# Two of eleven blocks of a down projection by seven products of squares

## What is computed

```python
def hybrid_layer(x, ...):
    h = rms_norm(x, g_attn_pre)
    proj = jnp.einsum('bsd,de->bse', h, w_in) + b_in
    # ... two groups of heads, each with its own mask and norm ...
    x = x + rms_norm(jnp.einsum('bse,ed->bsd', mix, w_out), g_attn_post)
    h = rms_norm(x, g_ffn_pre)
    f = jax.nn.silu(jnp.einsum('bsd,df->bsf', h, w_gate)) * jnp.einsum('bsd,df->bsf', h, w_up)
    x = x + rms_norm(jnp.einsum('bsf,fd->bsd', f, w_down), g_ffn_post)
    return x
```

## Time and profile before

| | |
|---|---|
| median of 3 runs | 571.66 us (571.55 to 571.73) |
| span of the profiled execution | 569.7 us |
| PE, weight loads, DVE, ACT, POOL busy | 99%, 81%, 66%, 52%, 40% |
| granted TensorE clock | 0.999 of full speed |
| loaded | 105.7 MB |

### The profile page before, as it was taken

How to read it: one execution, slowest core, us unless ns; L and a number is a source line. 1 busy time by engine, 2 the same in 40 slices (tenths; PEclk the granted TensorE clock), 3 DMA queues, 4 the chain that set the end, 5 groups by cost and what they waited for, 6 DMA issues and landing times.

```text
span 569.7 us, 8885 instructions
## 1 busy us (share of the span) xinstructions
PE 562.0 (99%) x3395; PEld 462.1 (81%) x3395; DVE 375.1 (66%) x487; ACT 294.0 (52%) x420; POOL 229.1 (40%) x451
## 2 busy tenths in 40 slices
PE   8999999999999999999999999999999999999996
PEld 5878878888888888888888878888888888888884
DVE  5799895946755746365597987775855746734622
ACT  6576684664445353263546748574645354425420
POOL 1101001507797797860120000033296797785000
PEclk9999999999999999999999999999999999999999
DMA  8954624538556461478266443525575455352701
GB/s 299 370 210 156 237 89 173 223 133 315 184 217 202 167 221 33 189 294 298 89 239 208 158 167 124 211 76 221 222 258 201 173 217 183 113 221 88 282 1 74
DMA packets 18730, 107.34 MB, mean 188 GB/s; under 512 B 2816, under 2 KB 3072, under 8 KB 7168
## 3 DMA queue, kind: packets, MB, share of 16 engines
q1 hardware_dynamic: 18688, 106.78, 50.8%
HBM read 105.72 MB, written 1.05 MB: 187 GB/s over the span
## 4 chain that ended last, share of the span: by engine, by line
PE 93%; DVE 3%; DMA 1%; ACT 1%; issue 1%; POOL 0%; SPq 0%; DVEq 0%; POOLq 0%
PE bank L1209 84%; PE bank L1249 4%; PE bank L1234 2%; PE bank L1275 2%; PE bank L1302 2%; DVE w_l L812 1%; DMA raw<-in_w_blocks 1%; ACT work L631 0%; DVE work L896 0%; DVE work L874 0%; DVE work L897 0%; DVE work L952 0%; DVE work L902 0%; DVE x L986 0%; ACT work L608 0%
## 5 line engine op out<-in xcount | busy, mean ns | idle before, releaser
L812 DVE TENSOR_TENSOR w_l<-raw,w_h 128x2048 fp32r<-128x2048 f32 x90 | 206.6, 2301 | 112.6 <-ACT w_h L559 112.4
L559 ACT ACTIVATE w_h<-raw 128x2048 fp32r<-128x2048 f32 x90 | 171.7, 1915 | 108.5 <-PE bank L1209 91.5
L1209 PE MATMUL bank<-w_h,actT_h 128*128 128x512 f32 (+1 forms) x568 | 223.9, 394 | 0.1
L517 POOL COPY work<-work 32x128 f32<-32x128 f32 (+1 forms) x384 | 191.3, 498 | 75.6 <-DVE work L1013 59.8
L1209 PE MATMUL bank<-w_h,actT_l 128*128 128x512 f32 (+1 forms) x568 | 219.9, 387 | 0.0
L1209 PE MATMUL bank<-w_l,actT_h 128*128 128x512 f32 (+1 forms) x568 | 219.4, 386 | 0.0
L1209 PEld LDWEIGHTS bank<-w_h,actT_h 128*128 128x128 f32 x568 | 106.8, 188 | 23.1 <-issue 2.5
L1209 PEld LDWEIGHTS bank<-w_h,actT_l 128*128 128x128 f32 x568 | 106.7, 188 | 22.1
L1209 PEld LDWEIGHTS bank<-w_l,actT_h 128*128 128x128 f32 x568 | 106.9, 188 | 20.1
L504 POOL TENSOR_TENSOR norms<-norms,constants 128x1 f32<-128x1 f32 x8 | 2.7, 342 | 131.7 <-ACT bank L658 131.7
L1209 PE MATMUL bank<-w_h,fT_h 128*128 128x512 f32 x160 | 49.4, 390 | 0.0
(11 more groups left out here) (78 smaller groups left out, 396.1 us busy)
## 6 DMA issues: line engine op xcount, KB each, us to landing
raw<-in_w_blocks SPq DMA_DIRECT2D x90, 1024.0 KB, 4.8
bias<-in_b_in SPq DMA_DIRECT2D x8, 256.0 KB, 6.1
raw<-in_w_blocks SPq DMA_DIRECT2D x4, 256.0 KB, 5.9
raw<-in_w_blocks SPq DMA_DIRECT2D x2, 512.0 KB, 8.6
x<-in_x SPq DMA_DIRECT2D x2, 512.0 KB, 10.7
gain_b<-in_g_attn_post SPq DMA_DIRECT2D x2, 512.0 KB, 7.3
bias<-in_g_ffn_pre SPq DMA_DIRECT2D x2, 512.0 KB, 7.4
gain_b<-in_g_ffn_post SPq DMA_DIRECT2D x2, 512.0 KB, 6.5
```

The costliest lines, as they stand in the source:

```text
L517: ins = nc.gpsimd.tensor_copy(crossed[t][32 * j:32 * j + 32, i * n:(i + 1) * n], squares[t][32 * i:32 * i + 32, j * n:(j + 1) * n])
L559: nc.scalar.activation(w["h"][:, slot(b), :], raw[:, r, :], ACT.Copy).then_inc(hi_ready, 1)
L812: nc.vector.tensor_tensor(w["l"][:, slot(b), :], raw[:, slot(b, RAW), :], w["h"][:, slot(b), :].bitcast(F32), ALU.subtract).then_inc(lo_re ...
L1209: ins = nc.tensor.matmul(bank[BANK_OF[name]][:, 0:n], left[s][:, at + k, tokens(t)], right[r][:, k, c * BANK:c * BANK + n], start=first an ...
```

## The change

A block of the down projection is X = A B with A of 2 x 2 tiles (tokens by k, 128 x 128) and B of 2 x 2 tiles (k by columns, 128 x 512). Strassen's scheme in Winograd's form makes X with seven products instead of eight, out of sums of tiles of A and of B. It is applied to the k-tiles 0 to 3 (chunk 0 of f), in two of the eleven blocks.

- The down blocks come in another order: k-tiles 4 to 9 (35 to 37), then the first fast block as two entries, `raw` (38: three tiles of B, high and low part of 1536 columns) and `sum` (39: four sums of tiles, 2048 columns), then k-tiles 10 to 13 (40, 41), the second fast block (42, 43), and 14 to 21 (44 to 47). There are 48 entries, 46 of them loaded; slots and raw buffers go round without leaving any out.
- DVE makes the sums of weights (`add_squares`) and of f (`add_s`, in chunk 1 of gate and up, with `hi_s` and `lo_s`). POOL's exchange of chunk 1 waits for `add_s`.
- PE accumulates four of the seven products straight in banks of the result or of their own, and three into banks 4 to 7 over both fast blocks. After the second, ACT copies one of them (`keep_m1`), and DVE joins them to the four banks of the result (`join_first`, `join_second`, eight operations in PSUM).
- PE's order at the end: half of block 44 for tile 1; tile 0 of 44, each bank once its join is made; 45 to 47 for tile 0; the rest for tile 1, with the next layer's transposes in the middle of 46.
- Some buffers move (silu and squares change places, the sums lie over the gains or the work buffer), and the next layer's `gain_a` is loaded later.

```diff
-BLOCKS += [("down", k, 2, 0, D) for k in range(0, KF, 2)]
+FAST = 2
+FAST_CHUNKS = FAST // 2
+BLOCKS += [("down", k, 2, 0, D) for k in (4, 6, 8)]
+RAW_AT = []
+for n in range(FAST):
+    RAW_AT += [len(BLOCKS)]
+    BLOCKS += [("raw", 2 * n, 2, 0, D), ("sum", 2 * n, 2, 0, D)]
+    if n == 0:
+        BLOCKS += [("down", k, 2, 0, D) for k in (10, 12)]
+FIRST_LATE = len(BLOCKS)
+BLOCKS += [("down", k, 2, 0, D) for k in (14, 16, 18, 20)]
...
@@ scalar
                 hi_f(L, FFN_CHUNKS - 2, 0)
+                after(L, FIRST_DOWN)
                 hi_f(L, FFN_CHUNKS - 2, 1)
-                for b in range(FIRST_DOWN, NB - 4):
+                for b in range(FIRST_DOWN + 1, NB - 4):
+                    if b == RAW_AT[FAST - 1]:
+                        keep_m1(L)
                     after(L, b)
-                    if b == FIRST_DOWN + 4:
+                    if b == RAW_AT[0] + 1:
                         hi_f(L, FFN_CHUNKS - 1, 0)
                         hi_f(L, FFN_CHUNKS - 1, 1)
...
@@ vector
+            def add_s(L, c):
...
+                nc.vector.tensor_tensor(s3, a11, a21, ALU.subtract)
+                link(L, nc.vector.tensor_tensor(s1, a21, a22, ALU.add))
+                link(L, nc.vector.tensor_tensor(s2, s1, a11, ALU.subtract))
+                nc.vector.tensor_tensor(s4, a12, s2, ALU.subtract).then_inc(s_added, 1)
...
+            def add_squares(L, n):
...
+                link(L, nc.vector.tensor_tensor(dst[:, 0, :].rearrange("p (a n) -> p a n", a=2),
+                                                raw[:, r, BANK:3 * BANK].rearrange("p (a n) -> p a n", a=2),
+                                                b12.unsqueeze(1).broadcast_to([P, 2, BANK]), ALU.subtract))
+                link(L, nc.vector.tensor_tensor(dst[:, 1, 0:BANK], dst[:, 0, BANK:2 * BANK], b11, ALU.add))
+                nc.vector.tensor_tensor(dst[:, 1, BANK:2 * BANK], b21, dst[:, 1, 0:BANK], ALU.subtract
+                                        ).then_inc(sums_ready, 1)
...
+                first, second = RAW_AT
+                lo_f(L, FFN_CHUNKS - 2, 0)
+                squares_f(L, FFN_CHUNKS - 1, 0)
+                add_squares(L, 0)
+                after(L, FIRST_DOWN)
+                lo_f(L, FFN_CHUNKS - 2, 1)
+                squares_f(L, FFN_CHUNKS - 1, 1)
+                after(L, FIRST_DOWN + 1)
+                after(L, FIRST_DOWN + 2)
+                after(L, first)
+                add_squares(L, 1)
+                after(L, first + 1)
+                lo_f(L, FFN_CHUNKS - 1, 0)
+                lo_f(L, FFN_CHUNKS - 1, 1)
+                after(L, first + 2)
+                after(L, first + 3)
+                join_first(L)
+                after(L, second)
+                after(L, second + 1)
+                join_second(L)
...
@@ tensor
+                product(m1, a11, b11, first, last)
+                product(x12, s4, b22, False, last)
+                product(x11, a12, b21, False, last).then_inc(block_used, 1)
+                pe.wait_ge(lo_ready, L * NB + b + 2)
+                ends = [product(m6, s2, t2, first, last), product(m5, s1, t1, first, last),
+                        product(m7, s3, t3, first, last)]
+                product(x21, a22, t4, False, last).then_inc(block_used, 1)
...
+                multiply(L, 1, FIRST_LATE, (0,), asks=True).then_inc(second_begun, 1)
+                multiply(L, 0, FIRST_LATE, asks=False, apart=True)
+                f_landed(L, FFN_CHUNKS - 2, 0)
+                multiply(L, 0, FIRST_LATE + 1)
+                multiply(L, 0, FIRST_LATE + 2)
+                f_landed(L, FFN_CHUNKS - 1, 0)
+                multiply(L, 0, FIRST_LATE + 3)
+                pe.wait_ge(joined, 4 * L + 4)
+                multiply(L, 1, FIRST_LATE, (1,))
+                multiply(L, 1, FIRST_LATE + 1)
+                multiply(L, 1, FIRST_LATE + 2, (0,))
+                if L < depth - 1:
+                    rows(L + 1, 0, 0)
+                multiply(L, 1, FIRST_LATE + 2, (1,))
+                f_landed(L, FFN_CHUNKS - 1, 1)
+                multiply(L, 1, FIRST_LATE + 3)
```

More of the change, by code:

```diff
@@ L70, with slot, before, load_count @@
 SLOTS = 4
[L71 to L83, removed]
+SUMS = 2
+def slot(L, b):
+    return (L * NB + b) % SLOTS
+def before(b):
+    return b - SLOTS
+def load_count(L, b):
+    return L * NL + LOADED.index(b)
+def raw_slot(L, b):
+    return load_count(L, b) % RAW
+def raw_done(L, b):
+    return (load_count(L, b) // RAW + 1) * 16
 def freed_by(b):
@@ L95, in completes @@
     m, k0, nk, col, n = BLOCKS[b]
-    if m == "down":
+    if m in ("down", "raw", "sum"):
         return [("down", t, c) for c in range(2)] if k0 + nk == KF else []
@@ L222, in trunk @@
         minus_half, eps = constants[:, 0:1], constants[:, 1:2]
-        junk = [[silu[t].bitcast(BF16) for t in range(T)], [rope_tmp.bitcast(BF16)] * T]
+        junk = [[squares[t].bitcast(BF16) for t in range(T)], [rope_tmp.bitcast(BF16)] * T]
         bank = [ctx.enter_context(nc.psum_tensor(f"bank{b}", [P, BANK], F32)) for b in range(8)]
+        products = [bank[b] for b in (4, 5, 6, 7)]
         x_in_done = [sem(f"x_in_done{t}") for t in range(T)]
@@ L394, in _ @@
             for L in range(depth):
-                for b in range(RAW + 1, NB):
+                for b in LOADED[RAW + 1:]:
                     load_block(L, b)
@@ L547, in hi @@
             def hi(L, b, wait=True):
[L549 to L550 removed]
+                m, k0 = BLOCKS[b][0:2]
+                if m == "sum":
+                    act.wait_ge(sums_ready, sums_done(L, k0 // 2))
+                else:
+                    r = raw_slot(L, b)
+                    act.wait_ge(raw_in[r], raw_done(L, b))
                 last = before(b)
@@ new lines, in join, with join_first @@
+            def join(L, t, c, what):
+                x = bank[BANK_OF["down", t, c]]
+                nc.vector.tensor_tensor(x[:], x[:], what, ALU.add).then_inc(joined, 1)
+            def join_first(L):
+                _, m6, m5, _ = products
+                dve.wait_ge(m1_kept, L + 1)
+                join(L, 0, 0, m1_sum)
+                dve.wait_ge(products_full, 3 * L + 1)
+                link(L, nc.vector.tensor_tensor(u2, m1_sum, m6[:], ALU.add))
+                dve.wait_ge(products_full, 3 * L + 2)
+                link(L, nc.vector.tensor_tensor(u4, u2, m5[:], ALU.subtract))
+                join(L, 0, 1, u4)
```

235 lines of the change are left out of this document (168 added, 67 removed).

## The result

| | before | after |
|---|---|---|
| median of the runs | 571.68 us | 580.70 us (580.26 to 580.92) |
| ratio | | 1.0158 (95% interval 1.0144 to 1.0173) |
| span of the profiled execution | 569.7 us | 578.5 us |
| PE, DVE, ACT, POOL busy | 99%, 66%, 52%, 40% | 97%, 70%, 52%, 44% |

The account below looks back on a forecast made before the run. PE's number of products was taken to bound the kernel. Waits of 2.3 + 2.2 us in layer 0 and 1.6 + 2.2 - 1.36 in layer 1 gave +6.9, taken as +6.8: 571.66 -> 578.5 us, range 570.2 to 581.5.

Parts of the forecast that it names:

- The products: PE, both layers: each fast block takes 21 products for 24, twelve fewer at 0.2267 us, 2.72 us in all.
- Layer 0's saving is worth nothing: Start of layer 1: PE reaches block 3 earlier by 1.36 us but waits for DVE's chain until the same 296.04.
- Rival 2: Exchange in time and layer 0's saving kept too, because DVE's chain moves: 568.9 us; chance 0.04.
- Rivals 3: Rival 3: PE alone counts, sums and joins cost two short waits of 0.5 us a layer: 571 to 575; chance 0.07.
- 4: Rival 4: block 40 and the exchange both late, over 581.5 us; chance 0.04.
- The hold-up of POOL by the new sums: Last exchange, down projection: 17 locked DVE instructions (24.1 us) hold up POOL's copies, adding 19.0 us to its 19.0.
- The short form of the sum: Last exchange's length from whole terms, less 0.3 for each passing copy: 38.0 us, ending at 259.5 and 536.6.
- Rival 1: Down projection: exchange in time as the new sums don't hold POOL up or run faster, 570.3 us; chance 0.15.
- The start of that group: Chunk 4's exchange starts about 1.7 us later in layer 0 and 2.6 in layer 1, from chunk 1's added work.
- The waits at 44: Down projection: block 44 ready at 264.8 and 542.3, wanted at 262.5 and 540.7; PE waits 2.3 and 1.6 us.
- The joins: Down projection, behind block 44: PE waits 1.5 us at the first join and 0.7 after, 2.2 in each layer.
- the likeliest case: Whole kernel: late exchange makes PE wait at block 44 and the joins, 578.5 us, bounds 575.5 to 580.5; chance 0.70.

Follow-up runs that it names:

- The transposes: Changed kernel with DVE's three sums of weights of each fast block made stream transposes of 1024, 512 and 512 columns: 574.25 us, ratio 1.0059.
- the edit that shortens the chain: Layer 1: block 3's low half before the rotation, its first products before projection 0's transposes; on changed kernel with f-late and drains-first edits 569.13 us, on kernel before 571.27.

## Why the prediction was right, and where not

- **The products** come at 0.2267 us, twelve less: right, and the run of six left out in layer 1 shows 1.15 of the 1.36.
- **Layer 0's saving is worth nothing**, since DVE's chain gates block 3 of layer 1: right, forecast as a gap of 1.3, measured 1.29, and shown by leaving six products out there (1.0001) and by the edit that shortens the chain only where the saving exists (0.9959 with it, 0.9998 without). Rival 2 is out. Rivals 3 (571 to 575) and 4 (over 581.5) are out by the time, 580.70.
- **The hold-up of POOL by the new sums**: right in kind and size. From the last group's start to the last copy I had 38.7 and 39.1 us, it takes 38.96 and 38.97. The transposes settle it: with them, the last group is 3.4 us shorter. The short form of the sum took 0.3 us off for each copy that passes where its test on layer 1 had taken 0.2; by the measured 38.96 it is (24.1 + 19.0 - 38.96) / 17 = 0.24. Of DVE's added work the prediction had some 18 us a layer; it is (405.7 - 375.1) / 2 = 15.3. Rival 1 is out; its price, about 571 for sums that don't hold POOL up, is not what that run shows (574.25), because the late start and the gap at the start stay with it.
- **The start of that group** is the term that was mis-sized: 1.7 and 2.6 us later by the forecast, 2.7 and 4.3 measured. I had priced what chunk 1's extra work costs there and taken it that the ring then goes on at its old pace. It doesn't: exchange, ACT's and DVE's halves of f, the product with silu and the transpose follow one another in a ring (18.4 to 19.0 us of copies and 3.39 to the next start) that is as long as PE's chunk of 21.8 us. In the kernel before, layer 1, it ran with it, 18.37 + 3.39. In the changed kernel each further chunk takes 22.4 us, so that lateness grows by 0.6 a chunk instead of going away. In layer 1 that makes 1.4 and 1.7 us from chunk 0 to 1 and from 1 to 2, where I had 1.3 and 1.2, and then 0.6 twice. The slower rhythm isn't the change's own, since the kernel before falls into it in some layers too; of the profiled kernels, each with the sums of f goes in it behind chunk 1 in both layers. Against a ring that keeps PE's pace (87.06 us) the changed kernel's last group is 4.7 us late in layer 0 as well; the 2.7 counts from a layer 0 that was itself 2.0 late. A low half of f of 0.77 us lies beside the second exchange there (at 213.46, in layer 0) and behind it in the kernel before (at 492.36, when the copies of the group of 474.22 were all but through). In layer 0 of the kernel before, which goes in the slower rhythm, it lies beside it too (at 214.11). That this is where the 0.6 comes from was not tried.
- **The gap at the start of the down projection** (2.11 and 1.75 us) is the step that is missing. I followed the late exchange forward to block 44 and not through DVE's queue in chunk 5, where the drains that PE needs stand behind two low halves that it doesn't need yet. The kernel before had 0.25 us from the drain's end to PE's load there, so a look at who ends last ahead of 225.79 would have shown that nothing covers it.
- **The waits at 44**: 2.3 and 1.6 forecast, 1.29 and 1.31 measured. The exchange ended later than I had it, at 260.72 for 260.2 in layer 0, but PE came later too, by what it had lost at the start. The run with the drains put first shows the sum to be nearly one quantity: 2.84 us idle there, 2.69 lost, where the changed kernel lost 3.40 in the two places. So what the missing step itself cost is about 1.0 us of the time; the rest of the 3.9 lost at the start is the late exchange met sooner.
- **The joins**: 1.5 and 0.7 forecast, 1.42 and 0.66 measured.
- **The sum**: 4.5 and 3.8 us of waits forecast, 5.48 and 5.14 measured; 0.70 of that is hidden by the early start of this execution. So 576.5 stood against a span of 578.5, and 578.5 against a median of 580.7; the profiled execution took 580.26, 1.8 above its span, and was the fastest shown.
- Of the bounds, the likeliest case's own upper end, 580.5, was too low by 0.2; it had no room for a place that the account left out. The wider range held, in part by luck: its upper end had been set for a late block 40, which PE didn't wait for here, and there was 0.8 us left of it.

## What to carry to other kernels

Ask of each added instruction on an in-order engine not what it costs but what stands behind it, and follow lateness through every queue that it enters, including the ones in which it was never seen: a wait that ends 0.25 us ahead of the bounding engine is no cover. Where a ring of engines is as long as the bounding engine's period, lateness stays, or grows with each turn as it did here, so what one turn is given too much is paid at the end of the stage. And a scheme that saves work on the bounding engine pays only where that engine's time is what the next stage waits for; here one half of the saving had to be fetched by a second edit, in another layer, that by itself was worth nothing, and the rest by putting late input behind the blocks that don't need it.

## What the runs showed of the hardware

- A plain copy by DVE from SBUF to SBUF holds POOL's copies up as an instruction with two inputs does, one passing for each, though it is done in 0.46 us for 512 columns where the two-input form takes 0.69. A stream transpose of 512 columns takes 0.73 and holds nothing up: eleven copies of POOL in 2.73 us beside three of them, against four in 2.70 beside three sums.
- After a pause of 0.8 to 2.3 us two of PE's loads follow each other at 0.10 to 0.12 us before the pitch of 0.23 is back, so an idle time in the profile isn't the time lost: 2.26 idle was 2.11 lost, 1.57 idle was 1.42.
- DVE's products of silu and up, with one input in PSUM and one in SBUF, let POOL pass: beside the two of 226.58 to 227.45 in the changed kernel its copies start at 226.86, 227.19 and 227.52, the undisturbed pitch of 0.33.
- Two idle times of PE of the same length can differ in what the clock does: in the run with the drains put first, 2.85 us in layer 1 were followed by a granted clock of 0.50 from 548.2 to 551.2 us (weight loads 0.42 us apart for 0.23), 2.84 us in layer 0 by 1.00.
- Executions of kernels that are the same up to there come to the down projection of layer 0 within 1.2 us of each other (last load ahead of it at 225.0 to 226.2 in four). A difference of that size between two profiled spans says nothing until one has looked where it arises.
